# Scores of the FoX attention on 64 partitions: two heads' queries in one tile, without the zero-padded copy

## What is computed

```python
def _fox_block(q, cq, q_pos, k, v, ck, k_pos):
    # q: (B, Q, H, Dh), k, v: (B, K, H, Dh); H = 8 heads of Dh = 64
    s = jnp.einsum('bqhd,bkhd->bhqk', q, k).astype(jnp.float32) * (HEAD_DIM ** -0.5)
    s = s + jnp.transpose(cq, (0, 2, 1))[..., :, None] - jnp.transpose(ck, (0, 2, 1))[..., None, :]
    causal = k_pos[None, :] <= q_pos[:, None]
    s = jnp.where(causal, s, -jnp.inf)
    p = jax.nn.softmax(s, axis=-1)
    return jnp.einsum('bhqk,bkhd->bqhd', p.astype(v.dtype), v)
```

## Time and profile before

| | |
|---|---|
| time, median of 3 runs | 2195.11 us (2194.28 to 2196.66) |
| the profiled execution's own time | 2194.29 us |
| its span | 2192.5 us |
| mean granted clock of TensorE | 0.903 of full speed |
| PE, weight loads, DVE, ACT, POOL busy | 88%, 45%, 40%, 21%, 10% of the span |
| the prompt's attention | 633.8 to 863.3 us, 229.5 us |

### The profile page before, as it was taken

How to read it: one execution, slowest core, us unless ns; L and a number is a source line. 1 busy time by engine, 2 the same in 40 slices (tenths; PEclk the granted TensorE clock), 3 DMA queues, 4 the chain that set the end, 5 groups by cost and what they waited for, 6 DMA issues and landing times.

```text
span 2192.5 us, 25291 instructions
## 1 busy us (share of the span) xinstructions
PE 1926.2 (88%) x8864; PEld 996.2 (45%) x8864; DVE 871.3 (40%) x2383; ACT 470.6 (21%) x899; POOL 217.6 (10%) x178
## 2 busy tenths in 40 slices
PE   3569899999988888887988888999999999999970
PEld 1146555555446666333546533444444444444440
DVE  4934631101335554222223623334344344443439
ACT  0122101210135454113023211111111111111122
POOL 0000000100000000030000001122221222212110
PEclk8679756899999998999997899999999999999985
DMA  7921001100112000444001628999999999999656
GB/s 282 366 78 44 22 1 51 70 0 1 48 36 79 1 1 20 131 159 144 0 1 48 201 74 332 350 380 375 374 383 371 381 376 360 358 374 383 215 166 237
DMA packets 99946, 398.64 MB, mean 182 GB/s; under 512 B 27055, under 2 KB 29779, under 8 KB 70108
## 3 DMA queue, kind: packets, MB, share of 16 engines
q1 hardware_dynamic: 80812, 327.81, 39.1%
q0 software_dynamic: 19008, 69.21, 12.0%
HBM read 333.88 MB, written 61.52 MB: 180 GB/s over the span
## 4 chain that ended last, share of the span: by engine, by line
PE 45%; issue 5%; DVE 3%; ACT 2%; DMA 1%; POOL 0%; POOLq 0%; SPq 0%; DVEq 0%; ACTq 0%
PE psum L1011 21%; PE psum L1022 10%; PE psum L865 5%; PE psum L990 3%; PE psum L1029 1%; PE psum L844 1%; PE psum L899 1%; PE psum L889 1%; PE psum L906 1%; PE psum L941 1%; DVE arena L1703 1%; DVE arena L1692 1%; DVE arena L1704 1%; DVE arena L1693 1%; DVE arena L1691 0%
## 5 line engine op out<-in xcount | busy, mean ns | idle before, releaser
L1011 PE MATMUL psum<-arena 128*32 128x512 f32 (+2 forms) x2016 | 464.3, 597 | 1.1 <-ACT arena L1957 1.1
L1011 PEld LDWEIGHTS psum<-arena 128*32 128x32 f32 (+2 forms) x2016 | 169.2, 139 | 242.1 <-issue 240.2
L1022 PE MATMUL psum<-arena,tail 128*32 128x512 f32 (+2 forms) x1000 | 231.6, 595 | 0.0
L1642 DVE TENSOR_TENSOR arena<-arena,psum 128x256 f32<-128x256 f32 x65 | 39.6, 610 | 339.9 <-ACT arena L1962 336.9
L2086 POOL DMA_INDIRECT moe_rows<-arena x64 | 101.7, 1589 | 575.6 <-DVE arena L1670 439.5
L1022 PEld LDWEIGHTS psum<-arena,tail 128*32 128x32 f32 (+2 forms) x1000 | 79.9, 138 | 105.3 <-issue 105.3
L713 PE MATMUL psum<-arena 128*128 128x512 f32 (+1 forms) x384 | 126.5, 493 | 0.0
L865 PE MATMUL psum<-arena 128*128 128x512 f32 (+1 forms) x288 | 124.3, 593 | 0.8 <-ACT arena L1888 0.5
L1962 ACT ACTIVATE arena<-psum 128x256 f32<-128x256 f32 x65 | 25.0, 384 | 444.9 <-PE psum L1011 444.9
L754 PE MATMUL psum<-arena 128*128 128x512 f32 (+2 forms) x192 | 86.8, 568 | 10.4 <-ACT arena L1818 10.4
L865 PEld LDWEIGHTS psum<-arena 128*128 128x128 f32 (+1 forms) x288 | 68.5, 239 | 55.3 <-issue 40.1
(11 more groups left out here) (481 smaller groups left out, 2440.6 us busy)
## 6 DMA issues: line engine op xcount, KB each, us to landing
arena<-in_w_exp_gate SPq DMA_DIRECT2D x66, 1024.0 KB, 20.1
arena<-in_w_exp_up SPq DMA_DIRECT2D x66, 1024.0 KB, 25.1
arena<-in_w_exp_down SPq DMA_DIRECT2D x66, 1024.0 KB, 22.5
arena<-in_w_ada SPq DMA_DIRECT2D x12, 2048.0 KB, 8.3
arena<-in_w_ada_final SPq DMA_DIRECT2D x4, 2048.0 KB, 8.8
arena<-in_cache_k SPq DMA_DIRECT2D x32, 256.0 KB, 3.9
arena<-in_cache_v SPq DMA_DIRECT2D x32, 256.0 KB, 3.0
arena<-moe_rows SPq DMA_DIRECT2D x16, 512.0 KB, 12.7
```

Of the source, the lines that this page charges most:

```text
L1011: ins = pe.matmul(slot[2 + par][lo:hi, :].rearrange("p (u n) -> p u n", u=2), xTs[:, par, k, lo:hi], gu, start=(k == 0), stop=(k == KD - 1))
L1022: ins = pe.matmul(slot[1][lo:hi, n * 512:(n + 1) * 512], hTs[:, k, lo:hi], down_ring[at][:, k * D + n * 512:k * D + (n + 1) * 512], start= ...
```

## The change

`qT` has one tile for each pair of heads, as `kT` has. The product of the scores takes, of both, the 64 partitions of its head: 0 to 63 for even heads, 64 to 127 for odd ones. ACT evicts a whole tile of queries at a time; the fill on POOL and its semaphore are gone, and ACT waits there for the slot `("YT", 8)` directly, which POOL did before. The copies to `q_bd` take 64 partitions each and write only these.

```diff
-        qT = arena(21536, H, T)
+        qT = arena(21536, KA, T)
...
-                    ins = pe.matmul(slot[it % 2][:, c0:c1], qT[:, h, i * P:(i + 1) * P], kT[:, h // 2, c0:c1], start=True, stop=True)
+                    ins = pe.matmul(slot[it % 2][:, c0:c1], qT[DH * (h % 2):DH * (h % 2 + 1), h // 2, i * P:(i + 1) * P], kT[DH * (h % 2):DH * (h % 2 + 1), h // 2, c0:c1], start=True, stop=True)
...
-                dlink(cp(q_bd[:, :, h // 2, h * CH:(h + 1) * CH], qT[:, h, SEQ:T].rearrange("p (b s) -> p b s", b=NSEQ)))
+                half = slice(DH * (h % 2), DH * (h % 2 + 1))
+                dlink(cp(q_bd[half, :, h // 2, h * CH:(h + 1) * CH], qT[half, h // 2, SEQ:T].rearrange("p (b s) -> p b s", b=NSEQ)))
...
-            act.wait_ge(q_zero, 1)
+
+            slots.wait_full(act, ("YT", 8))
             for n, (c0, c1) in enumerate(CHUNKS):
                 for j in range(KA):
                     full(act, ("Q", n, j))
-                    src = slot[2 + j % 2]
-                    for a in range(2):
-                        ins = f(qT[a * DH:(a + 1) * DH, 2 * j + a, c0:c1], src[a * DH:(a + 1) * DH, 0:c1 - c0], ACT.Copy, scale=DH ** -0.5)
-                    empty(ins, ("Q", n, j))
+                    empty(f(qT[:, j, c0:c1], slot[2 + j % 2][:, 0:c1 - c0], ACT.Copy, scale=DH ** -0.5), ("Q", n, j))
...
-            slots.wait_full(pool, ("YT", 8))
-            pool.memset(qT[:, :, :], 0.0).then_inc(q_zero, 1)
```

More of the change, by code:

```diff
@@ L446, in hymba_program @@
         m_zero = sem("m_zero")
-        q_zero = sem("q_zero")
         dve_step = sem("dve_step")
```

## The result

The changed kernel takes 2357.03 us (median of four runs, 2355.83 to 2361.81) against 2195.89 for the kernel before: a ratio of 1.0738, 95% interval 1.0719 to 1.0757, 161 us slower. The forecast was 2324, the range 2200 to 2350. Way and mechanism came out as forecast, the size did not: the rise is 161 us instead of 130, and the time lies 7 us above the range.

What follows compares the result with a forecast made beforehand. PE bounds the prompt's attention (229.5 us). At 1.2 GHz slots 307, spreads 24, changes of height 26 and 3 in the open make 360 us, +130: 2194.3 + 130 = 2324 us. Range 2200 to 2350.

Steps and rivals of the forecast that it cites:

- What bounds the stage: Prompt's attention, 229.5 us: PE bounds it, busy 201.4 us against 124.5 for DVE and 117.8 for ACT.
- the parts that cost nothing: Fill on POOL (7.36 us), 12 fewer Q evictions on ACT, query copies on DVE: all hidden or unchanged, zero.
- Passes with 64 rows are not shorter: Attention's logits keep the number, width and duration of their passes with 64 rows: zero change.
- The rival of a faster pass: 64-row logits passes in attention stream in half the time: 31 us less, minus 17 for height changes, 2180; chance 0.03.
- The clock: Few-row passes do less for the clock, so attention, starting at 1.2 GHz, stays there: slots 307 us, spreads 24.
- The Trainium skill, first weighing: Gate set by PE's busy share, not rows: attention's clock stays as before, 2206 (2197 to 2213); chance 0.19.
- The Trainium skill, second weighing: Array packing promises up to twice the rate for contractions of 64 or less; for attention's logits 2180, chance 0.03.
- Changes of height: Each of attention's 64 iterations goes 128, 64, 128 rows: 0.4 us a pair at 1.2 GHz, 26 us.
- The slots: At 1.2 GHz each attention head has 180 pass slots of 0.213 us, 38.3 us; eight heads 307, spreads 24 more.
- The waits of PE for the exponentials [...] vanish under the slower PE: Attention's 40 us of PE waits disappear at 1.2 GHz; only first softmax and last eviction stay open, 3 us.
- All later stages keep their length: Sign of being right: stages behind attention stay unchanged, while attention lasts near 360 us.
- a time above 2350: Sign: a stage behind attention has slowed, or the weights of the 64-row passes load in the open.

Runs made afterwards that it cites:

- The packing alone: The changed kernel, but the scores multiply all 128 partitions of the packed tiles, adding the scores of a pair's two heads: 2195.93 us, ratio 1.0001.
- changes of height alone: The kernel before with 128-row scores, plus a two-pass product over 64 partitions and 8 columns ahead of each iteration's scores: 2215.15 us, ratio 1.0087.
- full-height spreads: The kernel before, but the spreads of the cumulated gates multiply 128 partitions (120 of them zeros) instead of 8: 2190.65 us, ratio 0.9971.
- the paired orders: The changed kernel with 128-row spreads, a pair's heads by turns, their scores issued together: 2318.48 us; with the next iteration's exponentials ahead of the eviction, 2157.70.
- early exponentials: ACT takes the next iteration's exponentials before evicting the last result: in the changed kernel 2339.41 us, in the kernel before 2185.45.

## Why the prediction was right and wrong

- **What bounds the stage, the parts that cost nothing**: right. The packing alone gives a ratio of 1.0001.
- **Passes with 64 rows are not shorter**: right; 384-wide passes start 0.64 apart at 1.2 GHz. The rival of a faster pass fell as written: this order of heads puts no passes on opposite halves side by side.
- **The clock**: right for this kernel, 0.50 from end to end, and the cause is the scores' rows: with the scores alone changed it falls, with changes of height alone it does not, and with 128-row spreads the six drops behind spreads before are gone. The prediction's reading that passes with few rows do less agrees with all of them. It did not ask what the spreads add: with spreads of 128 rows (2212 to 2272 us) or with two blocks of full rows in a head (2216) the clock comes back in spite of 64-row scores. In the changed kernel three things meet: the start at 1.2, spreads over 8 partitions in each head, and 64-row scores. What the start alone is worth was not tested.
- **The Trainium skill, first weighing**: "TensorE: Matmul & The Clock Gate", Part 1, ties the gate to how busy PE has been. Busy share alone does not explain these rows: PE is busy for 358.73 of 378.50 us at 1.2 GHz in the changed kernel, and for 185.63 of 214.20 mostly at 2.4 with full-height spreads.
- **The Trainium skill, second weighing**: "TensorEngine Tiling (Array Packing)", Theoretical Speedup, promises up to twice the rate for a dimension of 64 or less. In the changed kernel the trace shows none of it (0.64 us between 384-wide passes at 1.2 GHz); once two passes on different halves stood next to each other, in the paired orders, 3.0 us of passes took 1.71.
- **Changes of height**: taken at 0.4 us a pair, measured 0.49: 31 us instead of 26. Late weights (0.16) show in full behind wide passes too; I had thought part of that covered.
- **The slots**: the sum had 331 us of them. The first weighing pass of an iteration takes half a slot, so they come to 64 x 0.107 = 6.8 less. This error and that of the changes of height nearly cancel, which was luck.
- **The step that failed: "The waits of PE for the exponentials [...] vanish under the slower PE", with 3 us left in the open.** The sum was 360 us for attention, it took 378.5. PE's matmul row stood idle for 20.9 us of them: 10.5 ahead of the transposes for the exponentials (18.3 before), and 10.4 ahead of the scores until ACT had copied a spread out of the slot (10.4 before). The prediction took all waits for waits for the exponentials and did not price the second kind, of which the earlier trace rows show one (1.32 us). With 20.9 us in place of 3, 5 more for changes of height and 6.8 less for slots the sum is 376; 2 us stay unassigned.
- **Why they stayed**: early exponentials took 14 us off attention and the whole idle time ahead of the transposes, so the order on ACT made that part. The exponentials stood in ACT's queue behind an eviction that itself waits for PE's weighing; ACT waited there 34.4 us before and 86.0 in the changed kernel. So this was no wait for independent work, which a slower PE hides in full; it shrank by less than half. That the copies of the spreads are late for the same reason is likely, since they stand behind the same eviction; the early exponentials did not touch it, and it was not tested.
- **"All later stages keep their length"**: wrong by 10.5 us, from the end of attention to the end of the kernel (1339.7 instead of 1329.2). The kernel with the scores alone changed has it too (1339.9), the one with changes of height alone (1330.2) and the one with the packing alone (1329.1) have not. The sampled sequences' attention had a clock of 0.87 instead of 0.92. That the drops of its clock fall elsewhere when attention ends at another moment is likely, since the kernel with full-height spreads lost 7 us there too; it was not tested and stays open. The prediction did name, for a time above 2350, a slower stage behind attention and weights loaded in the open; both are there.

The range was drawn from the terms that I had priced; the two that it put at nearly nothing, waits and later stages, were 28 us more, beyond the 26 us between forecast and upper end.

## What to carry to other kernels

Before halving the rows of a matmul, look at the granted clock of the stage and at which passes stand ahead of its returns: here zero padding was not waste but kept TensorE at 2.4 GHz, and half-height passes paid only when two on different halves were issued side by side. When an engine slows down, do not strike out a wait whose chain goes back through that same engine: here one such wait stayed as long as it was and one lost less than half.

## What the runs showed of the hardware

- At the same count of passes, spreads over 128 partitions instead of 8 removed the six drops of the clock behind spreads: 1.00 throughout between 645 and 838 us. Rows filled with zeros did as well as rows with data (2195.9 us with data, 2195.6 with zeros).
- With 128 rows in every pass the clock still fell three times in attention, each time after PE had waited 1.99 us ahead of the scores (four more such waits had no drop behind them).
- Nearly the same instructions ran at either level: one kernel took 2212 us in one run and 2272 in another, at mean clocks of 0.898 and 0.871, and its 64-row scores ran 88 us on end at 2.4 GHz.
- A change between 128 and 64 rows and back costs 0.49 us over bare slots at 1.2 GHz around passes over 128 weights, of which 0.16 are late weights. At 2.4 GHz no run isolates it: 64 pairs with 128 short passes made attention 14 us longer, with part of them in waits; the estimate from the spreads, 0.29 a pair, would be 18.6.
- Score passes of two heads on opposite halves overlap nearly fully: 1.71 us for 3.0 us of slots.
